# Four-layer block at 3x-split fp32: first slot of each column phase multiplied as plain fp32 inside the norm, delta rule's first chunk and the Sqrt table loads reordered

## The reference

```python
h = rms_norm(x, gain) * (1.0 + sc) + sh          # sc, sh, gt: cond @ w_mod[l] + b_mod[l], six parts per layer
y = mixer_block(h, ...)                          # first half: projection by columns, mixers, projection by rows
x = x + gt * rms_norm(y, gain)                   # layers 0 and 1; in layers 2 and 3: x + gt * y
...                                              # second half: h @ w_up, activation, @ w_down
```

```python
v_new = u_n - w_n @ state
o_n   = q_n @ state + a_n @ v_new
state = state * exp(gl_n) + k_n.T @ v_new        # the first state is zero
```

## Time and profile before

| | us |
|---|---|
| median of 3 runs | 1586.65 |
| lowest, highest run | 1584.5, 1594.41 |
| the profiled execution, its own time | 1593.05 |
| its span (first to last instruction) | 1591.2 |
| TensorE busy in it | 1513.8 (95%) |
| VectorE, ScalarE, GpSimd busy | 1086.8, 750.8, 406.1 |
| mean granted TensorE clock | 0.946 of full |

### The profile page before, as it was taken

One profiled execution on the slowest core, in us unless ns is written; L12 is line 12 of the kernel. 1 busy time (PEld: TensorE's weight loads), 2 busy tenths in 40 slices (PEclk: granted clock), 3 DMA queues, 4 the chain that ended last, 5 costly groups with the idle time before them and its releaser, 6 DMA issues.

```text
span 1591.2 us, 28263 instructions
## 1 busy us (share of the span) xinstructions
PE 1513.8 (95%) x12078; PEld 1487.8 (94%) x12078; DVE 1086.8 (68%) x1461; ACT 750.8 (47%) x1011; POOL 406.1 (26%) x391
## 2 busy tenths in 40 slices
PE   3999899999999999999898889999999999999998
PEld 3999899999899999999898779999999999999998
DVE  7878597796556488797676546876458667465544
ACT  3545365434645455534676334444344444354432
POOL 0123020594121020396000311200319512220022
PEclk8998899998899889999899988999989999999999
DMA  9773379796242449798252012877538655446550
GB/s 394 308 293 136 138 278 352 285 339 242 106 186 80 156 186 358 291 343 304 106 176 90 1 54 85 323 287 278 193 119 304 238 214 213 183 179 215 211 190 27
DMA packets 47211, 336.69 MB, mean 212 GB/s; under 512 B 5360, under 2 KB 5744, under 8 KB 6768
## 3 DMA queue, kind: packets, MB, share of 16 engines
q1 hardware_dynamic: 46224, 333.03, 56.1%
q10 hardware_dynamic: 864, 1.87, 0.3%
HBM read 333.83 MB, written 1.05 MB: 210 GB/s over the span
## 4 chain that ended last, share of the span: by engine, by line
PE 74%; issue 11%; POOL 8%; DVE 5%; ACT 1%; DMA 0%; ACTq 0%; POOLq 0%; DVEq 0%
PE PS L543 44%; PE PS L846 14%; POOL acts_hi_lo L769 4%; POOL acts_hi_lo L771 4%; PE PS L786 3%; PE PS L615 2%; DVE ring L449 2%; PE PS L1078 1%; PE PS L2377 1%; PE PS L1456 1%; PE PS L623 1%; PE PS L2055 1%; PE PS L1436 1%; DVE weights_hi_lo L438 1%; PE PS L1464 1%
## 5 line engine op out<-in xcount | busy, mean ns | idle before, releaser
L438 DVE TENSOR_TENSOR weights_hi_lo<-ring,weights_hi_lo 128x1024 fp32r<-128x1024 f32 x426 | 550.9, 1317 | 272.8 <-ACT weights_hi_lo L429 271.4
L429 ACT ACTIVATE weights_hi_lo<-ring 128x1024 fp32r<-128x1024 f32 x426 | 444.5, 1058 | 477.4 <-PE PS L543 270.1
L543 PE MATMUL PS<-hi,weights_hi_lo 128*128 128x256 f32 x3456 | 562.2, 285 | 14.1 <-ACT hi L658 12.1
L543 PEld LDWEIGHTS PS<-hi,weights_hi_lo 128*128 128x128 f32 x3456 | 480.5, 193 | 17.5 <-issue 14.6
L846 PE MATMUL PS<-acts_hi_lo,weights_hi_lo 128*128 128x256 f32 x3168 | 379.8, 281 | 1.3 <-DVE weights_hi_lo L438 1.1
L846 PEld LDWEIGHTS PS<-acts_hi_lo,weights_hi_lo 128*128 128x128 f32 x3168 | 376.4, 189 | 2.0 <-issue 1.3
L543 PE MATMUL PS<-lo,weights_hi_lo 128*128 128x256 f32 x1728 | 349.8, 284 | 0.0
L769 POOL CAST acts_hi_lo<-arena 128x256 fp32r<-128x256 f32 x142 | 132.3, 932 | 826.2 <-PE PS L846 440.2
L543 PEld LDWEIGHTS PS<-lo,weights_hi_lo 128*128 128x128 f32 x1728 | 270.6, 193 | 0.0
L449 DVE CUSTOM_DVE_ANT_0 ring<-ring,cond 128x1024 f32<-128x1024 f32 x192 | 253.3, 1358 | 0.0
L771 POOL TENSOR_TENSOR acts_hi_lo<-arena,acts_hi_lo 128x256 fp32r<-128x256 f32 x142 | 170.0, 1197 | 11.4
(11 more groups left out here) (360 smaller groups left out, 1142.7 us busy)
## 6 DMA issues: line engine op xcount, KB each, us to landing
ring<-in_stream_dram SPq DMA_DIRECT2D x313, 1024.0 KB, 4.9
constS<-in_const_dram SPq DMA_DIRECT2D x1, 1856.0 KB, 8.6
cond<-in_rows_dram SPq DMA_DIRECT2D x2, 512.0 KB, 5.1
arena<-in_x_dram ACTq DMA_DIRECT2D x1, 1024.0 KB, 12.4
smallS<-in_small_dram SPq DMA_DIRECT2D x1, 883.0 KB, 12.4
out_dram<-arena ACTq DMA_DIRECT2D x2, 256.0 KB, 2.5
out_dram<-arena SPq DMA_DIRECT2D x2, 256.0 KB, 2.8
constS<-in_const_dram SPq DMA_DIRECT2D x1, 320.0 KB, 13.8
```

The source lines that it names most:

```text
L429: act.activation(wsp[:, g % 2, 0, at:at + HALF], ring[:, n % RING, at:at + HALF], ACT.Copy).then_inc(*ready.one())
L438: dve.tensor_tensor(wsp[:, g % 2, 1, at:at + HALF], ring[:, n % RING, at:at + HALF], wsp[:, g % 2, 0, at:at + HALF].bitcast(F32), ALU.subt ...
L543: mm = pe.matmul(o, lhs, rhs, start=k + g + j == 0, stop=k == KD - 1 and j == 2, skip_group_check=True)
```

## The change

In each of the eight cols phases the first slot is no longer split. It is multiplied unsplit, as float32, by u = X times the features' factor (`mods[:, q+1]`), with the shift `mods[:, q]` as a 257th column, during the norm. Its 16 matmuls of 257 columns go to banks 0 and 2. The reciprocal root, spread to bank 7 (`R_BANK`, before bank 2), multiplies the products afterwards, and the 257th column is added: this gives the same slot result. The slot after it is the one that is split ahead. In the same functions: the Sqrt table is asked for by a one-column Sqrt at the head of `act_root`; the start's ScalarE scales u only when the mods are ready.

```diff
@@ merge / plan: the first slot is ("raw", g), used by "pe"
-        flat = [("pe" if c == "cmp" else "dve", s) for _, items in phases for c, s in items]
+        flat = [("pe" if c in ("cmp", "raw") else "dve", s) for _, items in phases for c, s in items]
+        def slot_to_multiply_raw():
+            n0 = state["consumed"]
+            state["split"], state["raw"] = 0, n0
+            state["consumed"] += 1
+            return n0
@@ norm_of, TensorE
             def pe_part(pe):
-                for u in range(len(UNITS)):
-                    unit_sums(pe, u, sq, 0, xsq, xsum)
-                spread(pe, r, 2, xr, rx)
+                def products(k):
+                    pe.wait_ge(*scaled_x.at(k + 2))
+                    for g, bank in enumerate(RAW_BANKS):
+                        mm = pe.matmul(PS[:, bank, 0:SEQ + 1], slot(raw, "cols")[:, k, g * P:(g + 1) * P], u[:, k, :],
+                                       start=k == 0, stop=k == KD - 1, skip_group_check=True)
+                    if k == KD - 1:
+                        mm.then_inc(used["pe"], 1)
+                wait_slot(pe, raw)
+                if mods_ready:
+                    for i in range(len(UNITS)):
+                        sums(i)
+                    spread(pe, r, R_BANK, xr, rx)
+                    for k in range(KD):
+                        products(k)
+                    return
+                for i in range(3):
+                    sums(i)
+                    products(i)
+                sums(3)
+                sums(4)
+                products(3)
+                products(4)
+                spread(pe, r, R_BANK, xr, rx)
+                for k in (5, 6, 7):
+                    products(k)
@@ norm_of, ScalarE
+            def scale_features(act, k):
+                act.activation(u[:, k, 0:SEQ], X[:, k, :], ACT.Copy, scale=mods[:, q + 1, k:k + 1]).then_inc(*scaled_x.one())
             def act_root(act):
+                act.activation(stat[:, 54:55], cst("one"), ACT.Sqrt)
+                if not mods_ready:
+                    act.wait_ge(*updated.at(1))
+                    act.activation(u[:, :, SEQ], mods[:, q, :], ACT.Copy).then_inc(*scaled_x.one())
...
+                    if not mods_ready:
+                        for k in tiles:
+                            scale_features(act, k)
             def act_scale(act):
+                if mods_ready:
+                    act.wait_ge(*mods_ready)
+                    act.activation(u[:, :, SEQ], mods[:, q, :], ACT.Copy).then_inc(*scaled_x.one())
+                    for k in range(KD):
+                        scale_features(act, k)
                 for k in range(KD):
                     act.wait_ge(*td.at(k + 1))
@@ gemm_phase, ScalarE, ahead of the splits of its slots
+                act.wait_ge(used["pe"], ordinal[raw][1])
+                for g, bank in enumerate(RAW_BANKS):
+                    act.activation(c[:, g, :], PS[:, bank, 0:SEQ + 1], ACT.Copy).then_inc(*copied.one())
@@ gemm_phase, VectorE, ahead of the splits of its slots
+                dve.wait_ge(*copied.at(2))
+                order(dve.tensor_tensor(c[:, :, 0:SEQ], c[:, :, 0:SEQ],
+                                        PS[:, R_BANK, 0:SEQ].unsqueeze(1).broadcast_to((P, 2, SEQ)), ALU.mult))
+                order(dve.tensor_scalar(f[:, 0:SEQ], c[:, 0, 0:SEQ], c[:, 0, SEQ:SEQ + 1], None, ALU.add))
+                dve.tensor_scalar(f[:, SEQ:2 * SEQ], c[:, 1, 0:SEQ], c[:, 1, SEQ:SEQ + 1], None, ALU.add).then_inc(*scaled.one())
@@ hyb_mixers, TensorE
-                pe.wait_ge(*wts.at(1))
-                pe.wait_ge(*qds.at(1))
                 for n in range(4):
                     if n:
                         pe.wait_ge(*sts.at(n))
+                        if n == 1:
+                            pe.wait_ge(*wts.at(1))
+                            pe.wait_ge(*qds.at(1))
@@ hyb_mixers, VectorE
                 split_lo(dve, slots[0], (0,))
-                dve.wait_ge(*up_.at(1))
-                split_lo(dve, slots[0], (1,))
+                dve.wait_ge(*us.at(1))
+                dve.tensor_copy(v4[0:64, :, 0, :], u4[0:64, :, 0, :]).then_inc(*vns.one())
                 dve.wait_ge(*wp_.at(1))
                 dve.tensor_copy(wT, bank2(4)).then_inc(*wts.one())
                 exponents(6)
...
                         if n == 0:
                             dve.tensor_copy(new, kv).then_inc(*sts.one())
+                            split_lo(dve, slots[0], (1,))
```

More of the change, by code:

```diff
@@ L25 @@
 PRE = 1
+RAW_BANKS = (0, 2)
+R_BANK = 7
 CW = SLOT // KD
@@ L54, in proj_slots @@
     if kind == "hyb":
-        starts = [2048] + [CW * i for i in range(6)] + [2056 + CW * i for i in range(4)] + [6 * CW, 7 * CW, 3080, 3336]
+        starts = [0, 2048] + [CW * i for i in range(1, 6)] + [2056 + CW * i for i in range(4)] + [6 * CW, 7 * CW, 3080, 3336]
         return [("cols", "hyb_w_in_2", 0, ((s, 8 if s == 2048 else CW),)) for s in starts]
@@ L100, in mods_beside, with merge @@
     return [23] if (kind, l) == ("up", 3) else []
-def merge(gemm, name):
+def merge(gemm, name, raw=0):
     mod = [s for q in mods_beside(name) for s in mod_slots(q)]
-    out, done = [("gemm", g) for g in gemm[:PRE]], 0
-    for i, g in enumerate(gemm[PRE:]):
-        upto = len(mod) * (i + 1) // (len(gemm) - PRE)
+    out, done = [("raw", g) for g in gemm[:raw]] + [("gemm", g) for g in gemm[raw:raw + PRE]], 0
+    gemm = gemm[raw + PRE:]
+    for i, g in enumerate(gemm):
+        upto = len(mod) * (i + 1) // len(gemm)
         out += [("mod", m) for m in mod[done:upto]] + [("gemm", g)]
@@ L347, in phase_slots @@
         def phase_slots(name):
-            n0, items = state["consumed"] - state["split"], items_of[name]
+            items = items_of[name]
+            n0 = state["consumed"] - state["split"] - (items[0][0] == "raw")
             state["consumed"] = n0 + len(items)
@@ L462, in mod_sums @@
                     order(dve.scalar_tensor_tensor(m, m, 1.0, p5[:, 1, :], ALU.add, ALU.add))
-                    order(dve.tensor_tensor(m, m, p5[:, 2, :], ALU.mult))
+                    ins = dve.tensor_tensor(m, m, p5[:, 2, :], ALU.mult)
+                    if done:
+                        ins.then_inc(*done.one())
+                    else:
+                        order(ins)
                 else:
@@ L489, in gemm_phase @@
             gemm, todo = slots_of(name)
-            n_pe = len(gemm)
+            n_pe = len(gemm) + 1
+            raw, c, f = state.pop("raw"), raw_taken(), raw_scaled()
+            copied, scaled = sig("raw_products_copied"), sig("raw_products_scaled")
             taken = sig("gemm_bank_taken")
@@ L520, in _ @@
                 work = pe_beside and pe_beside(pe)
-                for i, n in enumerate(gemm):
+                piece(work)
+                for i, n in enumerate(gemm, 1):
                     if i >= banks:
                         pe.wait_ge(*bank_taken(i - banks))
+                    if i == RAW_BANKS[1]:
+                        pe.wait_ge(*copied.at(2))
                     w_hi, w_lo = halves_of(n, "cols")
@@ L532, in _ @@
                         for j, (w, h) in enumerate(pieces(w_hi, w_lo, hi, lo)):
[L533 removed]
+                            if i == 1 and j != 1:
                                 pe.wait_ge(*(h_lo if j else h_hi)[k])
@@ L639, in pe_part, with sums @@
             def pe_part(pe):
-                for u in range(len(UNITS)):
-                    unit_sums(pe, u, sq, 0, xsq, xsum)
-                spread(pe, r, 2, xr, rx)
-            def act_root(act):
-                for u, tiles in enumerate(UNITS):
-                    act.wait_ge(*updated.at(u + 1))
-                    if u >= 2:
-                        act.wait_ge(*xsum.at(u - 1))
-                    act.activation(sq[:, u % 2, 0:len(tiles) * SEQ],
+                def sums(i):
+                    unit_sums(pe, i, sq, sums_bank, xsq, xsum)
@@ L651, in act_root @@
                                    X[:, tiles[0]:tiles[-1] + 1, :].rearrange("p k t -> p (k t)"), ACT.Square).then_inc(*xsq.one())
+                    if not mods_ready:
+                        for k in tiles:
+                            scale_features(act, k)
                 act.wait_ge(*xsum.at(len(UNITS)))
-                act.activation(r, PS[:, 0, 0:TT], ACT.Sqrt, bias=cst("eps"), scale=1.0 / D).then_inc(*xrt.one())
+                act.activation(r, PS[:, sums_bank, 0:TT], ACT.Sqrt, bias=cst("eps"), scale=1.0 / D).then_inc(*xrt.one())
@@ L1732, in proj @@
             def proj(blk):
-                gemm_phase(blk, ("proj", l), lambda i: 8 if i == 0 else (0 if i < 7 else 256), evac, beside=delta_inputs(Q, AB, SQ))
+                gemm_phase(blk, ("proj", l), lambda i: 8 if i == 1 else (0 if i < 7 else 256), evac, beside=delta_inputs(Q, AB, SQ))
             return proj, lambda blk: hyb_mixers(blk, l, Q, GT, SQ, VS, oT), oT
@@ L2186, in _ @@
                     rows = slice(64 * r, 64 * r + 64)
-                    if n == 0:
```

(3 more changed lines are left out.)

101 lines of the change are left out of this document (59 added, 42 removed).

## The result

The kernel after took 1604.59 us (median of 5 runs, 1601.3 to 1607.04) beside 1588.96 for the kernel before on the same chip (5 runs). The ratio is 1.0098, with a 95% interval of 1.0079 to 1.0117: slower by 15.6 us, just under 1%. Forecast were 1594 us and a difference of +7.6. The pair of profiled executions differs by less than the medians: 1601.3 against 1593.05, which is 8.3. So the traces are read for where the time goes, and the ratio for how much it is.

The account below looks back on a forecast made before the run. TensorE, with 74% of the chain of waits, was taken as the bound. Losses 3 x 3.2 + 10 + 3.5 less gains 8 and 7.5 gave +7.6 on the median 1586.65: 1594 us, own range 1586 to 1602, wide 1564 to 1612.

Parts of the forecast that it names:

- The normed transitions: Four at half clock from S (start of x sums): spread S+16.7, third slot S+26.5, 3.2 us lost each.
- The second condition: Transition to `proj` 1: its load waits for the plain slot, lands S+28; third slot S+33.6, 10 us lost, not 3.
- The short transitions: Three transitions at full clock: spread done S+8.9, third slot S+18.7, 2.7 us gained each, 8 together.
- The delta rule: First v_new ahead of w's copy: second chunk 3.5 us earlier, 4 more from the clock; 7.5 gained taken.
- The start: First projection: third slot at 51.0, 1.5 us lost, 2 more for layer 0's inputs; 3.5 together, between 1 and 6.
- the inputs of layer 0: At the start: issued at 46.2 behind the waiting load, landed about 59, needed at 56.8; 2 us lost.
- The sum: Whole kernel: 3 x 3.2 + 10 + 3.5 - 8 - 7.5 = +7.6 us, giving 1594 us against the median.
- what costs nothing: Eight fewer slots to split, bank and signal renames, and the extra one-column Sqrt: no time lost anywhere.
- rival B: Clock falls in the short transitions too, 1.5 us lost three times; delta chain keeps 3.5: +24, 1611 us, chance 0.22.
- A: Clock comes back by itself in normed transitions, 4.9 us gained in three, condition free; written 1568 us, chance 0.18.
- C: Waits on SyncE's queue hidden: without 8 of the condition's 10 and 2 of the start's 3.5, 1584 us, chance 0.12.

Follow-up runs that it names:

- Experiment 5: Kernel after plus six unread multiplications around the spread of y's root in each normed transition, ahead of the x sums; 1575.47 us, ratio 0.9913.
- Experiment 3: Kernel after with all x sums and the spread ahead of the plain products in the four normed transitions; 1592.42 us, ratio 1.0028.
- experiment 6: Kernel before plus six unread multiplications around the spread of y's root in each normed transition; 1580.66 us, ratio 0.9959.
- experiment 4: Kernel before with only the delta rule's reordering (first chunk's v_new ahead of w's copy); 1583.18 us, ratio 0.9966.
- Experiment 1: Kernel after with TensorE's wait for the plain slot moved behind the start's x sums and spread; 1597.39 us, ratio 1.0061.
- experiment 2: Kernel after with the second condition's transfer issued two phases earlier, its Silu left in place; 1599.09 us, ratio 1.0059.
- experiment 10: Kernel after with start wait moved, condition's transfer and Silu early, and three instead of five unread multiplications behind y's spread; 1578.15 us, ratio 0.9914.

## Why the prediction was right, and where it was not

**The normed transitions: right.** Spread done at S + 16.4 to 16.6 (forecast 16.7), third slot at S + 26.4, 26.3 and 26.2 (26.5), clock 0.50 in the alternation. Against before that is 2.6 to 3.1 us lost each, where 3.2 was the term. Experiment 5 turns "the clock costs it" from a reading into something shown: the same order at 1.00 gives S + 18.3. Experiment 3 shows the other half, that the products ahead of the spread carry the loss.

**The second condition: the wait right, its numbers in part by luck.** Landed at S + 29.1 (28), third slot S + 33.5 (33.6). The landing was 1.1 us late, and the table load of 1.28, which the forecast had behind the landing, was done ahead of it; the two errors cancel. The term of 10 had 2 us for a low clock behind the idle time. The slot behind it did take 7.55 us for 5.64, yet the stretch up to the next S is only 0.2 longer than before, so the term measured 7.9 to 8.1.

**The short transitions: right.** Spread at S + 8.5 (8.9), third slot at S + 18.3 (18.7), so 9.7 us in the three instead of 8. The clock stayed at 1.00.

**The delta rule: the mechanism right, the size of its clock part a matter of the execution.** From the end of the last product ahead of the chunk (928.4 before, 954.0 after) the second chunk's first product starts 2.1 us later, not 5.2: 3.1 us, forecast 3.5. Up to `up` 2's S the gain is 8.9, so the other 5.7 go with the clock, forecast 4, because the chunk after that runs at full clock as well. But that is this execution of before: held against experiment 6's trace of the old order the whole is 4.0 and what is not the earlier start 1.6. By the medians of experiment 4 the whole is 5.6.

**The start: wrong, and this is the step that failed.** The prediction had the plain products start at 36 "where the split ones did" and priced only what came behind: 1.5 for slower products, 2 for the inputs of layer 0. It named no wait ahead of the x sums. But `wait_slot(pe, raw)` is the first instruction of TensorE's part of the norm, the plain slot is the ninth of the stream (slot 8, behind the eight of the mods), and it lands at 30.5. Behind that wait stand the sums, the root, ScalarE's split of the following slot and, because VectorE's program holds the reciprocal ahead of the last mod slot, the last mod sums: VectorE idles 8.65 us for the root. The start lost 6.8 where 3.5 was the term and 6 its upper bound. Experiment 1 gives the forecast's start when only that wait is moved: 5.7 of the 6.8 are the wait. What is left, 1.1 at the third slot and 0.3 behind it, is less than the 3.5, because the 2 us for layer 0's inputs came out as nothing.

**The sum.** The traces give 8.3 where 7.6 was forecast, and that is luck in part: 3.3 too little for the start and 3.3 for the seven other stretches, which stood under what costs nothing, against 1.0 too much for the three normed transitions, 2.1 too much for the condition and 2.9 too little for the two gains. Most of the 3.3 lies in the stretches behind the third slots of `up` 0, `up` 1 and `proj` 3 (+0.7, +0.8 and +1.0); what makes them longer was not tried. The medians give 15.6, twice the forecast, and 1604.59 us lies above the forecast's own range of 1586 to 1602, within the wide one (to 1612) only because that makes room for rival B, which did not happen. What lies between 8.3 and 15.6 is in no step that was traced: before's profiled execution was 4 above its median, and after's 3 below its own. Part of it may be the delta rule, whose gain this pair shows 3 us larger than experiment 4's medians do. The forecast took off the 6.4 of the one and could not know the other.

**The rivals.** A fell as stated: under sums and plain products the clock came back only 16.1 to 16.5 us after S (at 213.2 in the transition to `up` 0), when the spread was all but done. The Trainium skill's rule ("TensorE: Matmul & The Clock Gate", section "HAM oscillation — how this bites in real kernels"), that filled gaps keep the clock, holds in experiment 5 and in after's short transitions, at 1.00. It does not hold in experiment 6, where the gap was filled too and the clock still fell 2.5 us behind S in two transitions. In after the gap, 2.36 us, is ahead of S, and the plain slot stood behind it. B fell: no short transition lost the clock. C fell for the condition, whose wait was on the path: experiment 2 took 5.5 us of it off. It held for layer 0's inputs, whose 2 us were hidden.

## What to carry to other kernels

Work put into a wait is worth what the clock allows: the same filling gained 3 us a transition where the clock was up at its start and lost 3 where it had just fallen, and six multiplications that nobody reads, in the gap ahead, moved four losses to gains. A part read from one pair of traces can be off by the clock of these two executions; look for the same stretch in the traces of other runs, as with the delta rule. A new wait belongs directly ahead of the first instruction that needs it. Look at every instruction, on every engine, that the waiting queue feeds, and at what lands when. And a reuse buffer that is released later delays not only its own reload but every transfer queued behind that reload.

## What the runs showed that I had not expected

The clock came back during 3.4 us of continuous multiplications of 256 columns (0.61 over 395.0 to 398.4, 1.00 from there), while 15.5 us of alternating sums of one column and products of 257 columns, also without a gap, left it at 0.50 in four transitions. Once at 1.00, the same alternating work kept it for its 7.9 us in the short transitions and in experiment 5. It looks as if the mixture held the level that it finds, but that is no rule: in experiment 10, with about 1 us idle just ahead of S, the mixture lost the clock in three transitions, and in experiment 6 the sums alone lost it in two with no idle time ahead. What decides was not tried. The other thing is the spread of the kernel before, 1578.7 to 1595.9 us over the runs of all comparisons, with a granted clock that differs from one execution to the next in stretches that no edit touched; effects below 5 us could not be read in the medians, and in the traces only where the stretch came out alike in several of them.
